# Building the compression blocks of a sparse-attention mixer on VectorE instead of GpSimd, and multiplying them in one column half of TensorE

## The reference, cut to what matters

```
n_cmp = (T - CMP_LEN) // CMP_STRIDE + 1                        # 15 windows of 32 tokens, 16 apart
cmp_idx = jnp.arange(n_cmp)[:, None] * CMP_STRIDE + jnp.arange(CMP_LEN)[None, :]
def compress(t, pe, w1, w2):
    blk = (t[:, :, cmp_idx] + pe).reshape(B, G, n_cmp, CMP_LEN * DH)
    return jax.nn.silu(blk @ w1) @ w2
k_cmp = compress(kc, pe_k, phi_k1, phi_k2)
v_cmp = compress(vc, pe_v, phi_v1, phi_v2)
```

## Time and profile before

| | us |
|---|---|
| median of 3 runs | 1723.05 (1722.67 to 1724.36) |
| the profiled execution's own time | 1724.36 |
| its span, from first to last instruction | 1722.6 |
| TensorE busy | 1632.4 (95% of the span) |
| VectorE busy | 1084.4 (63%) |
| ScalarE busy | 878.0 (51%) |
| GpSimd busy | 71.7 (4%) |

### The profile page before, as it was taken

One profiled execution on the slowest core, in us unless ns is written; L12 is line 12 of the kernel. 1 busy time (PEld: TensorE's weight loads), 2 busy tenths in 40 slices (PEclk: granted clock), 3 DMA queues, 4 the chain that ended last, 5 costly groups with the idle time before them and its releaser, 6 DMA issues.

```text
span 1722.6 us, 25059 instructions
## 1 busy us (share of the span) xinstructions
PE 1632.4 (95%) x9953; PEld 1400.8 (81%) x9953; DVE 1084.4 (63%) x1352; ACT 878.0 (51%) x1308; POOL 71.7 (4%) x134
## 2 busy tenths in 40 slices
PE   4989999998999989999998899999999998899997
PEld 4968888795888878888986788888888897688886
DVE  3776565678565666655656566567655665666554
ACT  4555444465554445444646454445444555554443
POOL 1000000020000002000002000002000001000000
PEclk9999999999999999999998999999999999999999
DMA  7504555540455557556450245556655442045551
GB/s 229 172 31 142 197 191 196 176 155 25 160 194 195 172 202 203 183 186 196 148 165 1 75 171 176 190 195 198 209 186 196 165 149 73 4 153 198 186 197 69
DMA packets 211150, 271.73 MB, mean 158 GB/s; under 512 B 4824, under 2 KB 191824, under 8 KB 211072
## 3 DMA queue, kind: packets, MB, share of 16 engines
q1 hardware_dynamic: 208528, 263.56, 45.9%
q0 software_dynamic: 2544, 7.09, 1.8%
HBM read 269.58 MB, written 1.05 MB: 157 GB/s over the span
## 4 chain that ended last, share of the span: by engine, by line
PE 88%; DVE 6%; ACT 3%; issue 1%; DMA 1%; SPq 0%; POOL 0%; DVEq 0%; POOLq 0%; ACTq 0%
PE pair L1686 29%; PE pair L1688 15%; PE bank L1643 12%; PE bank L1645 12%; PE bank L1644 12%; PE bank L1814 1%; PE pair L1795 1%; PE pair L1633 1%; PE bank L1844 1%; ACT probs L801 1%; DMA raw<-in_w_mem_kv 1%; DVE probs L1172 1%; PE bank L1761 1%; DVE negmax L1136 1%; DVE w_lo L1006 1%
## 5 line engine op out<-in xcount | busy, mean ns | idle before, releaser
L1686 PE MATMUL pair<-xt,w_hi 128*128 128x512 f32 x2112 | 750.2, 399 | 1.4 <-DVE xt L1015 1.4
L1006 DVE TENSOR_TENSOR w_lo<-raw,w_hi 128x2048 fp32r<-128x2048 f32 x248 | 568.0, 2290 | 161.1 <-ACT w_hi L679 159.1
L679 ACT ACTIVATE w_hi<-raw 128x2048 fp32r<-128x2048 f32 x248 | 474.3, 1914 | 294.6 <-PE pair L1688 200.5
L1688 PE MATMUL pair<-xt,w_lo 128*128 128x256 f32 x2112 | 592.8, 281 | 0.0
L1686 PEld LDWEIGHTS pair<-xt,w_hi 128*128 128x128 f32 x2112 | 397.6, 188 | 99.8 <-issue 2.1
L1688 PEld LDWEIGHTS pair<-xt,w_lo 128*128 128x128 f32 x2112 | 399.4, 189 | 2.3
L1643 PE MATMUL bank<-w_hi,xt 128*128 128x256 f32 x736 | 210.7, 286 | 0.4 <-DVE xt L1015 0.4
L1645 PE MATMUL bank<-w_lo,xt 128*128 128x256 f32 x736 | 208.2, 283 | 0.0
L1644 PE MATMUL bank<-w_hi,xt 128*128 128x256 f32 x736 | 208.2, 283 | 0.0
L1643 PE MATMUL bank<-w_hi,hid_hi 128*128 128x512 f32 x528 | 207.3, 393 | 0.0
L1645 PE MATMUL bank<-w_lo,hid_hi 128*128 128x512 f32 x528 | 206.4, 391 | 0.0
(11 more groups left out here) (242 smaller groups left out, 1422.9 us busy)
## 6 DMA issues: line engine op xcount, KB each, us to landing
raw<-in_w_gate_up SPq DMA_DIRECT2D x44, 1024.0 KB, 5.1
raw<-in_ffn_wg SPq DMA_DIRECT2D x44, 1024.0 KB, 5.1
raw<-in_ffn_wu SPq DMA_DIRECT2D x44, 1024.0 KB, 5.2
raw<-in_ffn_wd SPq DMA_DIRECT2D x44, 1024.0 KB, 5.0
raw<-in_w_in SPq DMA_DIRECT2D x30, 1024.0 KB, 5.2
raw<-in_w_down SPq DMA_DIRECT2D x22, 1024.0 KB, 5.0
raw<-in_w_o SPq DMA_DIRECT2D x8, 1024.0 KB, 5.2
raw<-in_w_out SPq DMA_DIRECT2D x8, 1024.0 KB, 5.3
```

The costliest lines, as they stand in the source:

```text
L679: act.activation(w_hi[s][:, :], raw[s][:, :], ACT.Copy).then_inc(hi_ready, 1)
L1006: dve.tensor_tensor(w_lo[s][:, :], raw[s][:, :], w_hi[s][:, :].bitcast(F32), ALU.subtract)\
L1686: pe.matmul(out[:, 512 * m:512 * (m + 1)], w[0][:, c, cols], xt[:, 2 * SEQ * c:2 * SEQ * (c + 1)], start=(c == 0), stop=False)
L1688: last = pe.matmul(out[:, 512 * m + SEQ:512 * (m + 1)], w[1][:, c, cols], hi_half(xt, c), start=False, stop=(c == KC - 1))
```

## The change

Three things change, in each of the two layers of the second block.

1. The 16 additions that build the blocks go from GpSimd's stream to VectorE's: the 8 for keys behind the copies of step 1, the 8 for values behind the maximum of step 2. The semaphore for them becomes `prep_ready`.
2. `cmp1` multiplies all of the keys' 16 matmuls, then all of the values' 16, and both write partitions 0 to 63 of the bank, in columns 0 to 29 and 30 to 59. It waits for the keys' blocks before the first and for the values' blocks in the middle.
3. silu works on 64 partitions by 60 elements in place of 128 by 30. The second weights lie side by side in partitions 0 to 63.

```
-            def blocks(l, w):                       # in GpSimd's stream
-                pool.wait_ge(heads_out_v.sem, heads_out_v.at((l, True, ("kc 1", "vc 1")[w])))
-                if w == 0:
-                    pool.wait_ge(task_out_v.sem, task_out_v.at((l, "pe")))
-                    pool.wait_ge(prep_ready.sem, prep_ready.at(("heads", l, "kw")))
...
-                            pool.tensor_tensor(
-                                b4[rows_, g, :, 8 * c:8 * c + 8], seg[:, g, :, :, q],
-                                term.unsqueeze(1).to_broadcast([HD, N_CMP, 8]), ALU.add)\
-                                .then_inc(blocks_ready.sem, blocks_ready.mark((l, w)))
...
+                def blocks(w):                      # in VectorE's stream
+                    dve.wait_ge(heads_out_v.sem, heads_out_v.at((l, True, ("kc 1", "vc 1")[w])))
...
+                                dve.tensor_tensor(
+                                    b4[rows_, g, :, 8 * c:8 * c + 8], seg[:, g, :, :, q],
+                                    term.unsqueeze(1).to_broadcast([HD, N_CMP, 8]), ALU.add)\
+                                   .then_inc(prep_ready.sem, prep_ready.mark(("blk", l, w)))
...
+                         (1, "end"): [lambda: blocks(0)], (2, "end"): [lambda: blocks(1)],
...
                     elif name == "cmp1":
                         for w in range(2):
-                            pe.wait_ge(blocks_ready.sem, blocks_ready.at((l, w)))
-                        for o in range(16):
-                            for w in range(2):
-                                last = pe.matmul(out[HD * w:HD * (w + 1), 0:30], phi1[w][:, HD * o:HD * (o + 1)],
+                            pe.wait_ge(prep_ready.sem, prep_ready.at(("blk", l, w)))
+                            for o in range(16):
+                                last = pe.matmul(out[0:HD, 30 * w:30 * w + 30], phi1[w][:, HD * o:HD * (o + 1)],
                                                  blk[w][:, 30 * o:30 * (o + 1)], start=(o == 0), stop=(o == 15))
...
-                    act.activation(hid_e[:, :], hid_e[:, :], ACT.Exp)\
+                    act.activation(hid_e[0:HD, :], hid_e[0:HD, :], ACT.Exp)\
...
-                    link(dve.tensor_scalar(hid_e[:, :], QT_B[:, 0:30], -1.0, 87.0, ALU.mult, ALU.min),
+                    link(dve.tensor_scalar(hid_e[0:HD, :], QT_B[0:HD, 0:60], -1.0, 87.0, ALU.mult, ALU.min),
...
-                    link(dve.tensor_scalar(hid_e[:, :], hid_e[:, :], 1.0, None, ALU.add))
-                    link(dve.reciprocal(hid_e[:, :], hid_e[:, :]))
-                    link(dve.tensor_tensor(hid_c[:, :], QT_B[:, 0:30], hid_e[:, :], ALU.mult),
+                    link(dve.tensor_scalar(hid_e[0:HD, :], hid_e[0:HD, :], 1.0, None, ALU.add))
+                    link(dve.reciprocal(hid_e[0:HD, :], hid_e[0:HD, :]))
+                    link(dve.tensor_tensor(hid_c[0:HD, :], QT_B[0:HD, 0:60], hid_e[0:HD, :], ALU.mult),
...
-                                             hid_c[HD:P, N_CMP * g:N_CMP * (g + 1)],
-                                             phi2[HD:P, 0:HD], start=True, stop=True)
+                                             hid_c[0:HD, 30 + N_CMP * g:30 + N_CMP * (g + 1)],
+                                             phi2[0:HD, HD:2 * HD], start=True, stop=True)
```

More of the change, by code:

```diff
@@ L306, in build @@
         pe_t = sb("pe_t", 2 * 16, at=m_base + 1248)
-        hid_c, hid_e = (sb(n, 30, at=m_base + 1376 + 256 * i) for i, n in enumerate(("hid_c", "hid_e")))
+        hid_c, hid_e = (sb(n, 60, at=m_base + 1376 + 256 * i) for i, n in enumerate(("hid_c", "hid_e")))
         lat_t = sb("lat_t", 6 * P, at=f_base + 23 * 1024)
@@ L421, in build @@
             sig(n) for n in ("heads_turned", "heads_out_a", "heads_out_v"))
-        blocks_ready = sig("blocks_ready")
         heads_out = {"scalar": heads_out_a, "vector": heads_out_v}
@@ L592, in _ @@
             load_gain(1)
-            def blocks(l, w):
-                pool.wait_ge(heads_out_v.sem, heads_out_v.at((l, True, ("kc 1", "vc 1")[w])))
-                if w == 0:
-                    pool.wait_ge(task_out_v.sem, task_out_v.at((l, "pe")))
-                    pool.wait_ge(prep_ready.sem, prep_ready.at(("heads", l, "kw")))
[L600 to L607, removed]
-                            pool.tensor_tensor(
-                                b4[rows_, g, :, 8 * c:8 * c + 8], seg[:, g, :, :, q],
-                                term.unsqueeze(1).to_broadcast([HD, N_CMP, 8]), ALU.add)\
-                                .then_inc(blocks_ready.sem, blocks_ready.mark((l, w)))
             def norm(j, source=squares):
@@ L652, in _ @@
                          a[f"nsa_phi_{which}1_2"][l].rearrange("(o p) n -> p o n", p=P)),
-                        (phi2[HD * w:HD * (w + 1), 0:HD], a[f"nsa_phi_{which}2_2"][l]),
+                        (phi2[0:HD, HD * w:HD * (w + 1)], a[f"nsa_phi_{which}2_2"][l]),
                         (pe_rows[0:16, P * w:P * (w + 1)],
@@ L662, in _ @@
                 power([(12, 14, A_QR), (14, 16, A_KVR)], ("latent", l))
-                for w in range(2):
-                    blocks(l, w)
                 for c in (6, 7):
@@ L1511, in places_out @@
                     link(dve.tensor_copy(pe_t[:, :], QT_B[:, 0:32]), task_out_v, (l, "pe"))
+                def blocks(w):
+                    dve.wait_ge(heads_out_v.sem, heads_out_v.at((l, True, ("kc 1", "vc 1")[w])))
+                    b4 = blk[w][:, :].rearrange("p (o g n) -> p g n o", o=16, g=B_G)
+                    for q in range(2):
+                        rows_ = slice(HD * q, HD * (q + 1))
+                        kc = kcv_t[:, SEQ * (2 * w + 1 - q):SEQ * (2 * w + 3 - q)].rearrange("p (g s) -> p g s", g=B_G)
+                        for c in range(2):
+                            seg = kc[rows_, :, 16 * c:16 * c + 240].rearrange("p g (n o l) -> p g n o l", o=8, l=2)
+                            term = pe_t[rows_, 16 * w + 8 * c:16 * w + 8 * c + 8]
+                            for g in range(B_G):
+                                dve.tensor_tensor(
+                                    b4[rows_, g, :, 8 * c:8 * c + 8], seg[:, g, :, :, q],
+                                    term.unsqueeze(1).to_broadcast([HD, N_CMP, 8]), ALU.add)\
+                                   .then_inc(prep_ready.sem, prep_ready.mark(("blk", l, w)))
                 def hidden_guarded():
                     dve.wait_ge(small_mm.sem, small_mm.at(("cmp1", l)))
-                    link(dve.tensor_scalar(hid_e[:, :], QT_B[:, 0:30], -1.0, 87.0, ALU.mult, ALU.min),
+                    link(dve.tensor_scalar(hid_e[0:HD, :], QT_B[0:HD, 0:60], -1.0, 87.0, ALU.mult, ALU.min),
                          prep_ready, ("cmp", l))
```

## The result

The changed kernel took 1735.64 us (median of 4, 1733.74 to 1735.92) against 1723.38 us (median of 4) for the kernel before: ratio 1.0068, interval 1.0051 to 1.0086, so 9 to 15 us slower where 4.9 were forecast and 1732.5 was the upper end of the range. Its profiled execution has a span of 1733.0 us, 10.4 more than before.

The account below looks back on a forecast made before the run. The prediction took TensorE's chain as the bound, GpSimd off it, cmp1 and silu open on it. Per layer 0.3 + 1.87 + 0.3 = 2.5 us, 4.9 for two: 1723.05 + 4.9 = 1728.0 us, 0.29% slower, range 1723.4 to 1732.5.

Parts of the forecast that it names:

- The additions: On VectorE, the keys' half ahead of scale(1) makes TensorE 0.3 us late at L1814 per layer; bounds 0 to 3.0.
- 1.4: Microseconds VectorE needs for the keys' eight additions, ahead of scale(1), at 0.18 us from start to start.
- 0.4: Microseconds regained on VectorE in L1162 and the two L1172 because GpSimd is idle: 0.19 + 0.24.
- 0.7: Microseconds of slack taken at TensorE's wait for scale(1) before L1814, from a span of 0.6 to 0.8.
- Rival D: TensorE's clock at the new wait: longer low stretch, 1734.9 or 1731.5 us, chance 0.09; no fall, 1724.7 or 1721.4, 0.05.
- The values' half: Eight additions on VectorE between step 2's maximum and scale(2): hidden, 0 us, with 1.3 us to spare.
- cmp1: All 64 passes in one column half at 0.058 us: 3.7 us instead of 1.86, +1.87 a layer; bounds 0 to 5.9.
- Rival A: In cmp1, pairs shared the load path, so one half costs nothing more: 1724.3 us, no measurable change; chance 0.14.
- Rival B: In cmp1, loads and matmuls don't overlap in one tile: +3.6 us a layer, 1731.4 us; chance 0.05.
- silu: Five instructions on the path, 60 elements long instead of 30: +0.3 us a layer; bounds 0.2 and 0.45.
- Rival C: Strided additions cost VectorE what they cost GpSimd, 0.51 us each: 5.8 us a layer, 1734.6 us; chance 0.07.
- The sum: Additions, cmp1 and silu: 0.3 + 1.87 + 0.3 = 2.5 us a layer, 4.9 us for two, giving 1728.0 us.

Follow-up runs that it names:

- the two kernels kept busy: Unread matmuls added in TensorE's waits: kernel before (2 ending step 0, 4 before scale(0)) 1720.64 us; changed kernel (also 3 before scale(1)) 1728.34 us.
- the additions alone: Kernel before with only the 16 additions moved to VectorE as in the change, cmp1 and silu untouched: 1728.19 us, ratio 1.0022.
- one half: Kernel before with cmp1 in one column half and silu on 64 x 60, additions left on GpSimd: 1729.71 us, ratio 1.0034.
- order: Kernel before, cmp1 still in two column halves, but all keys' matmuls first, then all values': 1727.86 us, ratio 1.0022.
- the run kept busy only up to `scale(0)`: Changed kernel with idle matmuls at the end of step 0 (2) and ahead of scale(0) (4), none ahead of scale(1): 1732.23 us, ratio 1.0051.
- the second interval of the changed kernel: From measuring the changed kernel once more, without alteration, on the chip of later runs: 1734.37 us, ratio 1.0061 (1.0047 to 1.0075).
- the rotation later: Kernel before with the gates and the window keys' rotation moved behind the maximum of step 2, scratch moved too: 1719.75 us, ratio 0.9975.
- both later: The kernel with gates and rotation moved later, plus additions on VectorE at the ends of steps 2 and 3: 1721.28 us, ratio 0.9988.

## Why the prediction was wrong

**What bounds the kernel.** Right for the kernel as it ran: GpSimd was not on the path, cmp1 and silu were open on it, and their delay reached the end one for one (kw to the end is 41.5 to 41.9 us in every kernel).

**The additions: this is the step that failed.** "So TensorE comes 1.4 - 0.4 - 0.7 = +0.3 us late." It came 0.8 us late, and behind the wait, where the sum has nothing, TensorE lost more again at the lower clock: 2.2 us a layer in all.
- 1.4 was 2.1. VectorE needed 2.06 to 2.11 us for eight, 0.26 from start to start and not 0.18. The overlap was there, 0.12 where I took 0.10; what was mis-sized is the price of one, 0.38 us in the median where I took 0.27 from the row of 128 x 128 elements. No run tells which part of the additions' pattern (64 partitions, the strides, the repeated operand) makes the difference.
- 0.4 was right. L1162 and L1172 of that step came back to 0.23 and 1.03 us.
- 0.7 held in the kernel as it ran: 2.1 - 0.4 - 0.7 = 1.0 us late, and the chain has 0.8. But it was the slack of a TensorE at half clock. With the clock full there is none, and the direct cost, read from the stretches of the two kernels kept busy (15.27 and 15.31 against 13.63), is about 1.65 us a layer, all of it at the wait.
- The clock stood in the sum with nothing. Rival D named it, but with 0.09 and as an accident. It was the rule: without fills the changed kernel and the additions alone took 16.89 to 18.17 us in six layers, on average 17.5; the kernels with the additions on GpSimd (before, one half, order) 13.96 to 15.93, on average 15.3. Of these 2.2 us, 0.9 lie ahead of the transposes L1809 (7.35 against 6.42 us on average) and 1.25 behind them (10.14 against 8.89). TensorE spent more time at the lower clock, 13.6 to 17.1 us of each stage in these six layers, against 6.8 to 13.7 in the other six. The wait itself brings the clock down, as the run kept busy only up to `scale(0)` shows.

**The values' half** was hidden, as forecast: `scale(2)` was done at 919.66, ahead of TensorE's L1809 at 921.52.

**cmp1.** Forecast +1.87, measured 3.71 - 1.86 = +1.85 us. Rival A is out (two passes did run at a time before). Rival B, by the rule of the Trainium skill on weight loads and row groups (TensorE: Matmul & The Clock Gate, Part 3), is out too: 64 passes with the same 128 rows took 0.058 us each, where load and matmul one after the other would have been 0.085 by the prediction's estimate. Here the trace and that rule differ. Not foreseen: going to one half is not needed for the loss; with both halves the order alone costs nearly the same, 3.50 - 1.86 = 1.64 us.

**silu.** Forecast +0.3, measured 2.11 - 1.85 = +0.26 us, the reciprocal 0.53 us on the chain.

**Rival C** (strides at GpSimd's price) is out: 0.26 us from start to start, not 0.51.

**The sum.** At full clock 2 x (1.65 + 1.85 + 0.26) = 7.5 us, and the two kept-busy kernels differ by 1728.34 - 1720.64 = 7.7 us. As run, 2 x (2.2 + 1.85 + 0.26) = 8.6 us, inside the second interval of the changed kernel (8.1 to 12.9 us) and just under the first (8.8 to 14.8). Part of the rest goes with the clock over the whole span. The mean granted clock of each execution is on record: 0.9795 on average in the ten executions of the changed kernel with a clock on record, 0.984 in the kernel before, 0.983 in the three kernels with one part of the change, 0.989 in both kept busy. Among the kernel before's own executions, those with a clock lower by 0.001 took 0.4 to 0.6 us longer (line fits to the three sets). By that, as an estimate, the 0.0045 between changed and before cost 1.9 to 2.7 us, which with the 7.5 to 7.7 of the kept-busy kernels makes 9.4 to 10.4 us, inside both intervals. What is left up to the medians of 10.4 and 12.3 us, and where in the span that clock was lost, stays open.

## What to carry to other kernels

Before you count slack ahead of a wait, look at the clock that the waiting engine had: slack of a TensorE at half speed is gone when it runs at full speed, and a chain "through TensorE" at half clock can be a chain through VectorE in truth. A wait that you add costs itself and can bring the clock down behind it: TensorE idle for 2.30 us at one place was followed by 3.4 us of low clock, which cost 1.6 us. Moved one step later, behind an instruction that waits anyway, the same 16 additions cost nothing that could be measured. If small matmuls are to run in two column halves, keep neighbours in the queue in different halves.

## What the runs showed of the hardware

- Idle matmuls in TensorE's waits kept the granted clock at 1.00 and made the kernel before 0.18% faster by the ratio (medians 1720.64 against 1724.49) and the changed one 6 to 7 us faster.
- The same unchanged stretch took from 13.63 us, all at full clock, to 15.93. Which part runs at the lower clock counts as well as how much: 3.4 us of it cost 1.6 us behind the wait for `scale(1)`, and about 0.1 in the first stage of the rotation later (64.97 against 64.87).
- GpSimd's additions slow VectorE's small fp32 instructions beside them. With both at work in the kernel with the rotation later, two of the six rotation steps of 32 elements took 0.48 and 0.37 us (the others 0.19 to 0.37):

```profile
912.42 0.48 DVE L1221 TENSOR_TENSOR junk<-proj,sin 128x32 f32<-128x32 f32 x1
912.94 0.37 DVE L1222 TENSOR_TENSOR junk<-proj,sin 128x32 f32<-128x32 f32 x1
```

  where the kernel before, with GpSimd idle, has 0.19 for it. The place in the stream and the scratch moved as well, but they are not the cause: with both later, where VectorE makes the additions and GpSimd is idle, all six steps at the same place took 0.19 us.
